# Two-layer encoder on one core: probabilities scaled on GpSimd before they are turned, in place of head outputs scaled by turned reciprocals

## What is computed

```python
# A: 128 queries against up to 3 blocks of 128 keys, 4 query heads, 2 key heads
scores = einsum(qb, kw) * hd ** -0.5 + bias            # ALiBi and window
probs = softmax(concatenate([scores, sink_col]))[..., :-1]
out_a = einsum(probs, vw)
# D: 128 queries against all 512 keys
out_d = einsum(softmax(einsum(q_blk, k) * hd ** -0.5), v)
...
mix = concatenate([rms_norm(o, g) for o in (out_a, out_b, out_c, out_d)])
h = layer_norm(DN_ALPHA * h + mix @ w_out, ln1_g, ln1_b)
```

## Time and profile before

| | us |
|---|---|
| median of 3 runs | 1061.21 (1061.2 to 1061.98) |
| the profiled execution | 1062.26 |
| its span | 1059.8 |
| PE busy in the span | 1044.2 (99%) |
| DVE / ACT / POOL busy | 774.9 / 538.8 / 117.2 |

### The profile page before, as it was taken

One profiled execution on the slowest core, in us unless ns is written; L12 is line 12 of the kernel. 1 busy time (PEld: TensorE's weight loads), 2 busy tenths in 40 slices (PEclk: granted clock), 3 DMA queues, 4 the chain that ended last, 5 costly groups with the idle time before them and its releaser, 6 DMA issues.

```text
span 1059.8 us, 15245 instructions
## 1 busy us (share of the span) xinstructions
PE 1044.2 (99%) x5281; PEld 868.3 (82%) x5281; DVE 774.9 (73%) x1075; ACT 538.8 (51%) x809; POOL 117.2 (11%) x122
## 2 busy tenths in 40 slices
PE   8999999999999999999999999999999999999997
PEld 6888887888888888888888888879888888888885
DVE  7845886868658757758887568777884784785687
ACT  3433666565265355355634247656634643652654
POOL 5200243200000000000002004331000000000003
PEclk9999999999999999999999999999999999999999
DMA  8432023031521521431333410211243134125122
GB/s 290 161 119 80 1 61 121 9 120 43 196 80 40 196 81 39 164 114 46 114 140 143 159 41 21 108 53 49 80 136 142 40 109 169 40 84 193 40 80 80
DMA packets 17378, 105.47 MB, mean 100 GB/s; under 512 B 2016, under 2 KB 2704, under 8 KB 5792
## 3 DMA queue, kind: packets, MB, share of 16 engines
q1 hardware_dynamic: 15984, 98.70, 26.0%
q0 software_dynamic: 1184, 5.86, 1.7%
q10 hardware_dynamic: 144, 0.07, 0.0%
HBM read 101.49 MB, written 2.10 MB: 98 GB/s over the span
## 4 chain that ended last, share of the span: by engine, by line
PE 93%; DVE 2%; issue 1%; POOL 1%; DMA 1%; ACT 1%; DVEq 0%; SPq 0%; POOLq 0%; ACTq 0%
PE bank L466 18%; PE bank L467 18%; PE bank L468 18%; PE bank L814 9%; PE bank L815 9%; PE bank L813 9%; PE bank L754 2%; PE bank L739 1%; PE bank L475 1%; PE bank L645 1%; PE bank L646 1%; DVE mx L1562 1%; DMA x<-in_x 1%; PE bank L542 1%; POOL x L1922 1%
## 5 line engine op out<-in xcount | busy, mean ns | idle before, releaser
L466 PE MATMUL bank<-h_hi,w_hi 128*128 128x512 f32 (+1 forms) x688 | 257.8, 375 | 0.0
L467 PE MATMUL bank<-h_lo,w_hi 128*128 128x512 f32 (+1 forms) x688 | 257.5, 374 | 0.0
L468 PE MATMUL bank<-h_hi,w_lo 128*128 128x512 f32 (+1 forms) x688 | 257.4, 374 | 0.0
L813 PE MATMUL bank<-w_hi,hid_hi 128*128 128x512 f32 x448 | 174.4, 389 | 0.0
L815 PE MATMUL bank<-w_hi,hid_lo 128*128 128x512 f32 x448 | 174.3, 389 | 0.0
L814 PE MATMUL bank<-w_lo,hid_hi 128*128 128x512 f32 x448 | 174.3, 389 | 0.0
L1259 DVE TENSOR_TENSOR w_lo<-w_raw,w_hi 128x2048 fp32r<-128x2048 f32 x62 | 141.9, 2288 | 39.2 <-ACT w_hi L929 32.7
L929 ACT CAST w_hi<-w_raw 128x2048 fp32r<-128x2048 f32 x56 | 107.2, 1914 | 85.3 <-PE bank L815 61.5
L467 PEld LDWEIGHTS bank<-h_lo,w_hi 128*128 128x128 f32 x688 | 129.6, 188 | 23.2
L466 PEld LDWEIGHTS bank<-h_hi,w_hi 128*128 128x128 f32 x688 | 129.5, 188 | 23.2
L468 PEld LDWEIGHTS bank<-h_hi,w_lo 128*128 128x128 f32 x688 | 129.5, 188 | 22.8
(11 more groups left out here) (183 smaller groups left out, 1632.1 us busy)
## 6 DMA issues: line engine op xcount, KB each, us to landing
w_raw<-in_weights SPq DMA_DIRECT2D x63, 1024.0 KB, 4.8
w_third<-in_weights SPq DMA_DIRECT2D x23, 1024.0 KB, 4.8
rows<-in_rows POOLq DMA_DIRECT2D x4, 1024.0 KB, 5.0
w_raw<-in_weights SPq DMA_DIRECT2D x4, 512.0 KB, 9.1
out_h<-x SPq DMA_DIRECT2D x8, 256.0 KB, 2.0
x<-in_x SPq DMA_DIRECT2D x3, 512.0 KB, 10.8
dft<-in_dft SPq DMA_DIRECT2D x2, 512.0 KB, 7.2
qk_gain<-in_qk_gain POOLq DMA_DIRECT2D x3, 192.0 KB, 3.3
```

The costliest lines, as they stand in the source:

```text
L466: pe.matmul(dst, s_hi, m_hi, start=first, stop=False)
L467: pe.matmul(dst, s_hi, m_lo, start=False, stop=False)
L468: return pe.matmul(dst, s_lo, m_hi, start=False, stop=last)
L813: pe.matmul(bank[dst + t][:], s_hi, m_hi, start=start, stop=False, skip_group_check=goes_on)
```

## The change

The probabilities of a unit are multiplied by their reciprocal row sums, per row, in place, by GpSimd, and only then transposed. Widening, turning, copying and multiplying by turned reciprocals go, with their buffers; squares, high and low parts read the values' bank. The reciprocals are made per pair on VectorE, behind the side adds of the step. The sink's score is put as one more column beside a unit's scores, so the exponential's row sum contains it. The maximum is written negated by one instruction (the factor 1/8 of group D moves to the copy of the queries). A quad's low part moves a step later, and `sum_quad` waits for it. In the tail, two of the four last side products move ahead of the turn of pair 15, and the transposes of tile 1 ahead of the sum of quad 7. GpSimd's work is written in a loop over steps; block 13's low part now is in step 11.

```diff
@@ PE
-                def turn_inverse(q):
-                    wait(pe, l, "inv_widened", q + 1)
...
                 def sum_quad(q):
                     wait(pe, l, "out_square_added", q + 1)
+                    wait(pe, l, "mix_lo", 2 + q + 1)
...
                 def turn_probs(u):
-                    wait(pe, l, "probs", u + 1)
+                    wait(pe, l, "scaled", u + 1)
...
-                    if quad_scaled_in(p) is not None:
-                        turn_inverse(quad_scaled_in(p))
-                    if quad_high_in(p) is not None:
-                        sum_quad(quad_high_in(p))
+                    if quad_low_in(p) is not None:
+                        sum_quad(quad_low_in(p))
                     for u in pair(p - 1):
                         turn_probs(u)
                 wait(pe, l, "probs", UNITS)
                 turn_half(l, 1, 0, 0)
                 take_values(PAIRS - 2)
+                last_sides = list(sides_of(PAIRS))
+                side(last_sides[0])
+                side(last_sides[1])
                 for u in pair(PAIRS - 1):
                     turn_probs(u)
                 sum_quad(6)
                 turn_half(l, 1, 0, 1)
                 take_values(PAIRS - 1)
-                turn_inverse(7)
-                last_sides = list(sides_of(PAIRS))
-                side(last_sides[0])
-                side(last_sides[1])
+                turn_stream(1)
                 sum_quad(7)
-                turn_stream(1)
                 side(last_sides[2])
                 side(last_sides[3])
@@ ScalarE
-                        act.activation(sink_e[:, quad, i:i + 1], cols[:, COL_SINK + head:COL_SINK + head + 1], ACT.Exp,
...
-                        act.activation(stage[:, u % STAGES, 0:n], stage[:, u % STAGES, 0:n], ACT.Exp, bias=bias,
+                        act.activation(stage[:, u % STAGES, 0:n + 1], stage[:, u % STAGES, 0:n + 1], ACT.Exp, bias=bias,
...
-                    act.activation(head_square[:], head_out[:, q % 2, :], ACT.Square).then_inc(sems["out_square"], 1)
+                    act.activation(head_square[:], bank[4 + q % 2][:, 0:GROUP], ACT.Square).then_inc(sems["out_square"], 1)
...
                     if quad_high_in(p) is not None:
+                        square_head_out(quad_high_in(p))
                         mix_high_quad(quad_high_in(p))
-                    if quad_scaled_in(p) is not None:
-                        copy_inverse(quad_scaled_in(p))
@@ VectorE
+                def invert_pair(p):
+                    b, i = (p // 2) % 2, 2 * (p % 2)
+                    wait(dve, l, "probs", 2 * p + 2)
+                    if p >= 4:
+                        wait(dve, l, "scaled", 2 * (p - 4) + 2)
+                    dve.reciprocal(inv[:, b, i:i + 2], p_sum[:, b, i:i + 2]).then_inc(sems["inv_denom"], 1)
...
-                        dve.reduce_max(mx[:, sl], bank[u % 2][:, 0:n], AX_X).then_inc(sems["row_max"], 1)
-                        wait(dve, l, "row_max", u + 1)
-                        dve.tensor_scalar(neg_mx[:, sl], mx[:, sl], -HEAD_DIM ** -0.5, None, ALU.mult).then_inc(sems["neg_max"], 1)
+                        dve.tensor_reduce(neg_mx[:, sl], bank[u % 2][:, 0:n], AX_X, ALU.max, negate=True).then_inc(sems["neg_max"], 1)
...
                 for p in range(PAIRS):
+                    if quad_low_in(p) is not None:
+                        mix_low_quad(quad_low_in(p))
...
-                    if quad_high_in(p) is not None:
-                        mix_low_quad(quad_high_in(p))
-                    if quad_inverted_in(p) is not None:
-                        invert_quad(quad_inverted_in(p))
-                    if quad_scaled_in(p) is not None:
-                        scale_quad(quad_scaled_in(p))
+                    if p < PAIRS - 1:
+                        invert_pair(p)
...
-                invert_quad(7)
                 mix_low_quad(6)
+                invert_pair(PAIRS - 1)
                 normalise_first(l, 1)
                 mean_quad(6)
-                scale_quad(7)
@@ GpSimd
+                def scale_probs(u):
+                    _, _, _, _, k0, k1 = unit(u)
+                    b, i = (u // 4) % 2, u % 4
+                    wait(pool, l, "inv_denom", u // 2 + 1)
+                    p_ = stage[:, u % STAGES, 0:(k1 - k0) * P]
+                    pool.tensor_scalar(p_, p_, inv[:, b, i:i + 1], None, ALU.mult).then_inc(sems["scaled"], 1)
...
+                for p in range(PAIRS):
+                    if quad_mean_in(p) is not None:
+                        quad_power(quad_mean_in(p))
+                    if quad_low_in(p) is not None:
+                        add_quad_squares(quad_low_in(p))
+                    if p == PAIRS - 1:
+                        layer_norm_rstd(2 * l + 1, 1, 2)
+                    scale_probs(2 * p)
+                    scale_probs(2 * p + 1)
...
+                    if p == 8:
                         wait(pool, l, "w_lo", 12)
                         split_low(l, 12)
-                    if q == 3:
+                    if p == 10:
                         load_rows(2 * l + 1)
-                    if q == 4:
+                    if p == 11:
                         split_low(l, 13)
+                    if p == 13:
+                        layer_norm_rstd(2 * l + 1, 0, 1)
+                add_quad_squares(6)
+                quad_power(6)
...
```

118 lines of the change are left out of this document (37 added, 81 removed).

## The result

The changed kernel takes **1082.99 us** (median of 4 runs, 1082.7 to 1083.87) against 1061.2 us before: a ratio of 1.0205, with a 95% interval of 1.019 to 1.022. The profiled execution has a span of 1080.9 us, 21.1 more than before, and its mean granted clock is 0.989 instead of 0.999. The forecast of 1068.3 us had the sign right and a third of the size; the time lies above the range of 1063 to 1077.

The account below looks back on a forecast made before the run. TensorE's work plus its waits was taken to bound the kernel. Per layer -1.3 (turns) + 3.6 (step 12) + 0.75 (step 14) + 0.5 (tail) = +3.55 us, +7.1 for two: 1068.3 us, range 1063 to 1077.

Parts of the forecast that it names:

- What bounds the kernel, and where it would break: Attention: TensorE's work plus its waits set the time; quad 4's sum in step 12 would wait 3.6 us for GpSimd.
- the 3 to 5 that were named: Sign: TensorE waits 3 to 5 us for GpSimd's sum of squares in step 12 of both layers, its longest wait.
- below 2: Sign: a TensorE wait below 2 us in step 14, where 0.75 us was forecast at quad 5's sum.
- The price of one product: GpSimd, 512 columns by a per-row scalar: 0.7 us, with 0.62 and 1.30 kept as ends.
- The walk through GpSimd's queue: GpSimd's in-order queue, instruction by instruction: TensorE waits 3.6 us in step 12, 0.75 in step 14, none in step 10.
- Turns saved: TensorE, steps 3 to 13: six quads without turned reciprocals at 0.22 us each, 1.3 us a layer gained.
- The small edits and the tail: Shorter VectorE and ScalarE work costed at nothing; the last two output products of attention start 0.5 us later a layer.
- the overlap: Tail: VectorE's normalisation of tile 1 takes turns with GpSimd's last two products and a sum, 1.8 us on top.
- The dear product: Rival: a GpSimd product costs as much as two inputs, 1.30 us and more; 1076.7 us; chance 0.17, 0.04 above 1080.
- Faster: Rival: GpSimd delivers quad 4's sum before 172.3, leaving only TensorE's saving, -3.0 a layer; 1055.2 us; chance 0.05.
- the later waits close: Rival: step 12's wait makes the gaps of step 14 and the tail disappear; +0.6 a layer, 1062.4 us; chance 0.10.
- Products above 1.5 us: Sign: GpSimd products costing this much in the profile after would make the prediction too low.

Follow-up runs that it names:

- the run with the cheap form: Changed kernel with its GpSimd products in the two-input form, the reciprocal read as a broadcast tile: 1071.6 us, ratio 1.0095.
- Filling the waits: Changed kernel with 9, 36 and 18 extra identity transposes on TensorE ahead of the quad sums in steps 10, 12 and 14: 1075.9 us, ratio 1.014.
- the mixed run: Changed kernel, block 13's low part at the end of step 14, pairs 0 to 7 multiplied on GpSimd in two-input form, 8 to 15 on VectorE: 1067.3 us.
- the small edits: Kernel before with only negated maxima, the sink as a column of the scores, and factor 1/8 in the copy of the queries: 1058.5 us, again 1058.4.
- mixed version: Changed kernel, low part in step 11, products of pairs 0 to 7 on GpSimd in two-input form, 8 to 15 on VectorE: 1060.9 us, ratio 0.9996.

## Why the prediction was wrong, step by step

- **What bounds the kernel, and where it would break: right.** TensorE's own work plus new waits; the longest wait is at quad 4's sum in step 12 of both layers, with L1769 just ended before it. At 5.09 us it lies just above the 3 to 5 that were named, and step 14's 2.67 above the "below 2". One distance is misread in the texts ahead, without effect on the sum: layer 1 follows 520.7 us behind layer 0, not 620.7 (696.20 - 175.52), so the second stretch of the earlier trace rows holds only the second half of its attention, and some of the MLP. From 630 to 726 us TensorE was busy for 94.74 of 96 us at the full clock.
- **The price of one product: the step that failed.** I took 0.7 us, near the price of a copy, and stated 0.62 to 1.30; it was 1.55, above the upper end. The nearest row above (1.30) was a subtraction of two tensors, and I took it as a ceiling without a row that made it one. The form with a scalar for each row is dearer: 1.55 us for 512 columns, 0.92 for 256, while the two-input form with a broadcast took 1.02, below that same 1.30. The Trainium skill (GPSIMD Engine Reference, Engine selection) has one-input work at roughly line rate; the trace disagrees for this product, with 3.0 ns a column, so the measurement decides. The range took over the mistake: its upper end, 1077, was worked out with 1.30.
- **The walk through GpSimd's queue: right, only its size was off.** The same walk with 1.55 a product gives 5.3 us in step 12 (measured 5.09; forecast 3.6), 2.5 in step 14 (2.67; 0.75) and 1.6 in step 10 (1.48; 0). With 1.02 a product it gives 4.2, 1.4 and no wait; the run with the cheap form has 3.99, 1.40 and none. Measured against forecast, the three waits are 1.5, 1.9 and 1.5 us too long: 4.9 of the 7.3 us a layer that were missing.
- **The slow clock: not in the forecast at all.** It was read as 1.00 and taken as given, a term put at nothing without a reason. Filling the waits gave back 6.1 us in the two attentions, 3.1 a layer.
- **Turns saved: right.** 1.3 forecast; 1.4 in the mixed run against the kernel before, 1.3 against the small edits.
- **The small edits and the tail: too high.** Edits costed at nothing are worth 1.0 us a layer, in the last steps. There the forecast was 0.5 longer; measured without a slow clock they are 0.5 to 0.6 shorter (25.46 with the waits filled and 25.38 with cheap products, against 25.94). The term that was mis-sized is the overlap, put at 1.8 us. VectorE in the changed kernel, tile 1's normalisation beside the products of pair 15:

```profile
200.01 1.83 DVE L1292 SCALAR_TENSOR_TENSOR x<-x,moments,rows 128x512 f32<-128x512 f32 x2
201.76 1.84 DVE L1301 SCALAR_TENSOR_TENSOR x<-x,rstd,rows 128x512 f32<-128x512 f32 x2
...
205.36 0.16 DVE L1467 TENSOR_SCALAR mean_sq<-bank 128x1 f32<-128x1 f32 x1 [1.76 <-PE bank L714]
```

  It took 3.59 us instead of 2.85, 0.7 more, and then VectorE stood 1.76 us for TensorE, so the overlap wasn't even in the way. (Nor do the prediction's own terms give the 1.3 us that it names for the tail without the overlap, since the overlap enters with 1.8.) Against the small edits the tail by itself still costs 0.5. That the move of two products is free only together with the shorter chain of quad 7, the forecast did not see: alone it costs 7 us a layer.
- **Rivals.** The dear product was one, with 0.21 in all, and its mechanism was the right one, but priced at 1.30 it ended at 1076.7. "Faster" and "the later waits close" both failed: the waits of steps 12 and 14 stand one behind the other. "Products above 1.5 us" was named as what would make the forecast too low, and it did.

Summed for a layer: -1.3 + 1.5 + 5.1 + 2.7 + 3.1 - 0.5 = 10.6, twice 21.2, against 21.6 in the two attentions of the profiled executions and 21.8 between the medians. Against the forecast, 4.9 us a layer come from the price, 3.1 from the clock, and the tail takes 1.0 off: 7.0 of 7.3.

What stays open: that the clock follows from idle time is shown by one run that fills it; how much idle time brings it down was not measured, and the same two waits brought it down in one layer and not in the other. Which instructions of VectorE GpSimd holds up was read where they happened to meet, not tried one by one. A mixed version with a tail as short as that of the small edits would, as an estimate from the two parts, be near 1057.4 us (60.32 + 24.90 against 61.17 + 25.94, 1.9 us less in each layer); it was not found.

## What to carry to other kernels

Work that is given to an engine with a queue in order costs nothing on average and still sets the end, if it stands ahead of something small that another engine waits for: walk the queue instruction by instruction, and list every reader, not only the first. Price an instruction by a row of the same form; where there is none, the nearest row is no ceiling, and one look at the form alone is cheap beside the loss. Ask of each new place for a long GpSimd instruction what VectorE does at that time, and put the slower clock behind a new wait of TensorE into the sum: here a wait of 2.7 us brought 1.3 us on top, and one of 5.1 us 1.6 in one layer and 2.1 in the other.

## What the runs showed of the hardware

- On GpSimd a multiplication of 128x512 numbers by a scalar for each row takes 1.55 us, the same product with the scalar broadcast as a second operand 1.02, a subtraction of two full tiles 1.30. On VectorE the first takes 0.44 to 0.49 us.
- A GpSimd subtraction over two SBUF tiles (4.5 us) held up VectorE's instructions with two tensors from SBUF (1.41 to 6.48 us) and its product with one (0.88 to 2.89 us) for nearly as long as it lay beside them. Beside the same subtraction row maxima read from PSUM (1.29 us for two, elsewhere 1.28), adds of a PSUM bank to an SBUF tile (0.75) and statistics of one SBUF tile (0.69) kept their length.
- Behind waits of 2.67 and 5.09 us TensorE's granted clock went to 0.50 for some us; behind a single wait of 1.40 or 1.48 us it stayed at 1.00. Behind 0.71 and 0.56 us one after the other it fell to 0.51 in layer 0 and stayed at 1.00 in layer 1 of the same execution.
